# The weight sums of the first block of a retention and sliding-window kernel: made by GpSimd instead of VectorE

## The reference

```python
h = x @ ret_w_in                       # (2048, 6144): q, k, v, g
q, k = rope(q), rope(k) / 16           # 4 heads of 256
att = (q @ k.T) * dec                  # chunks of 64
r = att @ v + (q @ state) * xi         # v: 4 heads of 512
state = state * g_chunk + (k * zeta).T @ v
r = (r - mean(r)) * rsqrt(var(r) + GN_EPS)
x = post_norm(x, (silu(g) * r) @ ret_w_out)        # retention layer

kv = x @ swa_w_kv                      # one K/V, 4 heads of 64
q, gate = split(x @ swa_w_in)          # 16 heads of 64
p = softmax_with_sink(q @ k_band.T / 8 + bias)
x = post_norm(x, ((p @ v_band) * silu(gate)) @ swa_w_out)   # window layer
```

## Time and profile before

| | |
|---|---|
| median of 3 runs | 2483.75 us (2483.28 to 2490.3) |
| the profiled execution | 2483.47 us, its span 2481.5 us |
| PE, DVE, ACT, POOL busy | 2341.3, 1812.3, 1180.6, 345.5 us |
| share of the span | 94%, 73%, 48%, 14% |
| mean granted TensorE clock | 0.982 |

### The profile page before, as it was taken

How to read it: one execution, slowest core, us unless ns; L and a number is a source line. 1 busy time by engine, 2 the same in 40 slices (tenths; PEclk the granted TensorE clock), 3 DMA queues, 4 the chain that set the end, 5 groups by cost and what they waited for, 6 DMA issues and landing times.

```text
span 2481.5 us, 30993 instructions
## 1 busy us (share of the span) xinstructions
PE 2341.3 (94%) x11506; PEld 1900.2 (77%) x11506; DVE 1812.3 (73%) x2578; ACT 1180.6 (48%) x1754; POOL 345.5 (14%) x352
## 2 busy tenths in 40 slices
PE   7889989989999999999999999999999999999995
PEld 5677777867778887787778888778777888878774
DVE  6977888755886668874697767886478667787457
ACT  3433345346544445534744544443664445553473
POOL 4212201113001110001201001100110110010122
PEclk9999999999999999999999999999999999999998
DMA  9786677571764445744274544575146444464413
GB/s 331 280 294 246 226 240 254 170 280 52 241 199 148 135 129 173 263 148 136 91 268 134 170 158 131 168 256 185 62 153 237 131 141 154 128 203 134 131 60 110
DMA packets 215061, 443.38 MB, mean 179 GB/s; under 512 B 15040, under 2 KB 52432, under 8 KB 211328
## 3 DMA queue, kind: packets, MB, share of 16 engines
q1 hardware_dynamic: 200832, 375.58, 46.1%
q0 software_dynamic: 14080, 65.83, 7.2%
HBM read 379.75 MB, written 57.41 MB: 176 GB/s over the span
## 4 chain that ended last, share of the span: by engine, by line
PE 58%; DVE 15%; issue 12%; DMA 7%; ACT 4%; POOL 2%; SPq 1%; POOLq 0%; DVEq 0%; ACTq 0%
PE accs L644 16%; PE accs L645 15%; PE accs L646 15%; DVE w_lo L1250 5%; DMA stage<-t_prep 4%; PE bank L644 2%; PE bank L646 2%; PE bank L645 2%; ACT w_hi L948 2%; PE bank L866 1%; DMA x_sums<-part_lo 1%; PE bank L875 1%; PE bank L885 1%; PE bank L730 1%; POOL rstd L1830 1%
## 5 line engine op out<-in xcount | busy, mean ns | idle before, releaser
L1250 DVE TENSOR_TENSOR w_lo<-stage,w_hi 128x1024 fp32r<-128x1024 f32 x536 | 670.4, 1255 | 414.3 <-ACT w_hi L948 413.2
L948 ACT ACTIVATE w_hi<-stage 128x1024 fp32r<-128x1024 f32 x536 | 563.6, 1057 | 585.3 <-DMA stage<-t_prep 273.3
L644 PE MATMUL accs<-w_hi,xs 128*128 128x512 f32 x1120 | 450.5, 402 | 45.2 <-DVE krT L1328 12.0
L646 PE MATMUL accs<-w_hi,xs 128*128 128x512 f32 x1120 | 442.6, 395 | 0.0
L645 PE MATMUL accs<-w_lo,xs 128*128 128x512 f32 x1120 | 442.4, 395 | 0.0
L644 PEld LDWEIGHTS accs<-w_hi,xs 128*128 128x128 f32 x1120 | 214.1, 191 | 100.1 <-issue 51.5
L644 PE MATMUL accs<-x_hi,w_hi 128*128 128x512 f32 (+1 forms) x640 | 248.8, 389 | 17.4 <-DVE qT L1714 16.3
L1830 POOL TENSOR_TENSOR rstd<-ve,half 128x1 f32<-128x1 f32 x96 | 80.7, 841 | 1265.1 <-DVE ve L1306 1215.5
L646 PEld LDWEIGHTS accs<-w_hi,xs 128*128 128x128 f32 x1120 | 213.7, 191 | 46.3
L645 PEld LDWEIGHTS accs<-w_lo,xs 128*128 128x128 f32 x1120 | 214.1, 191 | 42.5
L645 PE MATMUL accs<-x_lo,w_hi 128*128 128x512 f32 (+1 forms) x640 | 239.9, 375 | 0.0
(11 more groups left out here) (184 smaller groups left out, 3863.9 us busy)
## 6 DMA issues: line engine op xcount, KB each, us to landing
stage<-t_prep SPq DMA_DIRECT2D x224, 512.0 KB, 4.4
stage<-ret_w_in SPq DMA_DIRECT2D x96, 512.0 KB, 3.9
stage<-ret_w_in SPq DMA_DIRECT2D x128, 256.0 KB, 2.9
stage<-swa_w_in SPq DMA_DIRECT2D x64, 512.0 KB, 3.8
t_prep<-t_buf POOLq DMA_DIRECT2D x28, 1024.0 KB, 6.3
stage<-ret_w_out SPq DMA_DIRECT2D x48, 512.0 KB, 3.7
cs<-rope_t SPq DMA_DIRECT2D x16, 1024.0 KB, 7.6
t_buf<-ret_w_in POOLq DMA_DIRECT2D x32, 512.0 KB, 9.6
```

The lines of the kernel that those rows point to most:

```text
L644: mm(dst, lhs[0], rhs[0], start=start, stop=False, skip_group_check=reopened)
L646: return mm(dst, lhs[1], rhs[0], start=False, stop=stop, skip_group_check=reopened)
L948: copy(w_hi[:, g % HS], stage[:, g % LS], ACT.Copy).then_inc(w_hi_made, 1)
L1250: nc.vector.tensor_tensor(w_lo[:, g % LS], stage[:, g % LS], w_hi[:, g % HS].bitcast(F32), sub).then_inc(w_split, 1)
```

## The change

The sums leave VectorE's program. GpSimd makes them with its own TENSOR_TENSOR, with the same operands, in the slot in which VectorE made them, and the store stands right behind each in the same slot instead of one slot later.

```diff
@@ block.vector
-            def make_t(n):
-                b = t_buf[T_BUF[n]]
-                dve.wait_ge(t_loaded[T_BUF[n]], 32 * T_NTH[n])
-                link(nc.vector.tensor_tensor(b[:, 1, 1, :], b[:, 1, 1, :], b[:, 0, 1, :], sub))
-                link(nc.vector.tensor_tensor(b[:, 0, 1, :], b[:, 0, 1, :], b[:, 0, 0, :], sub))
-                link(nc.vector.tensor_tensor(b[:, 0, 0, :], b[:, 1, 1, :], b[:, 0, 0, :], add))
-                nc.vector.tensor_tensor(b[:, 1, 0, :], b[:, 1, 0, :], b[:, 0, 0, :], sub).then_inc(t_made, 1)
...
-                    if s == 0:
-                        for n, _, _, at_slot in T_PLAN:
-                            if at_slot == p:
-                                make_t(n)
@@ block.gpsimd
+            def make_t(n):
+                b = t_buf[T_BUF[n]]
+                pool.wait_ge(t_loaded[T_BUF[n]], 32 * T_NTH[n])
+                link(tt(b[:, 1, 1, :], b[:, 1, 1, :], b[:, 0, 1, :], sub))
+                link(tt(b[:, 0, 1, :], b[:, 0, 1, :], b[:, 0, 0, :], sub))
+                link(tt(b[:, 0, 0, :], b[:, 1, 1, :], b[:, 0, 0, :], add))
+                tt(b[:, 1, 0, :], b[:, 1, 0, :], b[:, 0, 0, :], sub).then_inc(t_made, 1)
...
                         for n, _, at_slot, made in T_PLAN:
                             if at_slot == p:
                                 load_t(n)
-                            if made + 1 == p:
+                            if made == p:
+                                make_t(n)
                                 store_t(n)
```

## The result

The kernel after takes 2520.21 us (median of 4 runs, 2517.09 to 2526.72); the kernel before took 2483.52 beside it (4 runs, 2477.35 to 2490.3). The ratio is 1.0151, with a 95% interval of 1.0132 to 1.0171. The sign was right, the size almost three times too small, and 2520 lies above the range (2474 to 2512).

A forecast was written before the change was run, and what follows sets the result against it. TensorE bounds block 1; block 0 runs slower, with VectorE's sums and waits for DMA as suspects. The terms 16 + 5 + 0 + 4 + 2 - 8 - 6 = +13 on 2483.5 us gave 2497 us, range 2474 to 2512.

The forecast's parts named there:

- Start: Sets 0 to 3, made behind GpSimd's x sums, store set 3 late and delay TensorE's weights: +16 us.
- The blocking: GpSimd's SBUF reads and VectorE's two-input instructions run in turns; at the start it moves set 3's store from 56 to 62.5.
- the 10 named: Sign of being right: TensorE's wait before P6's second pair is over 10 us.
- Set 14: Made behind a GpSimd gate, its store lands later and ScalarE's copy_r waits 10 us or more: +5 us.
- Set 20: In the heads, its store now stands ahead of an inverse root and a gate, 0 to 2 us earlier: 0.
- Inverse roots: GpSimd's roots in block 0 come 0 to 3 us late in three or four places: +4 us.
- The third rival: GpSimd becomes the bound: late inverse roots in all heads, 3 to 5 us in ten places; 2520 us, chance 0.10.
- Transfers: Sets 9 to 11 and 14 to 16 are stored later, into the next head's loads: +2 us, bounds -3 and +6.
- VectorE in the heads: Twenty sets leave VectorE; of 3.0 us each, 1.5 to 2 return as blocking: -8 us, bounds 0 and -25.
- Last four: Sets 24 to 27 in the q slots are stored earlier and shorten TensorE's wait at the q copy: -6 us.
- DVE busy: Sign of being right: VectorE's busy time at about 1,750 to 1,780, not 1,728, because blocked time is counted.

The follow-up runs named there:

- h_after_store_later: The kernel after, with each set's store one slot later, as in the kernel before; 2518.3 us, ratio 1.0138.
- q_pool_nosums: s_heads_pool with the sums of sets 4 to 23 left out; GpSimd only waits for the loads and stores; 2487.44 us, ratio 0.9999.
- n_nosums: The kernel before, with VectorE's sums of sets 4 to 23 left out, loads and stores kept; 2474.31 us, ratio 0.9953.
- s_heads_pool: The kernel after, but only sets 4 to 23 made by GpSimd, the others by VectorE; 2500.16 us, ratio 1.0056.
- s_first4_dve: The kernel after, but sets 0 to 3 stay with VectorE, sets 4 to 27 on GpSimd; 2500.1 us, ratio 1.006.
- m_noread: s_heads_pool with four GpSimd memsets that read nothing in place of each set's sums, for sets 4 to 23; 2486.92 us, ratio 1.0018.

## Why the prediction was right in sign and wrong in size

**Start: right.** +16 forecast, +17.1 measured alone. The store of set 3 was forecast at 62.5 and came at 64.72; the wait behind it was 16.8 us, over the 10 named. The blocking, read from the earlier trace rows, was needed for that: without it the store comes at 58.

**Set 14: right that it costs, the size not settled.** +5 forecast; moving the set earlier wins 6.4 with real sums and 15.4 with memsets, and a part of either is the wait that the kernel before had too. From slot 38 to slot 48 the kernel after loses 7.1 us against the kernel before. The wait itself did not grow past 10 as written (7.97, from 6.75), since TensorE and ScalarE were late by then too; the cost showed in slots, not in the wait's row. Set 20, priced at 0, had a gain that was overlooked: ScalarE's wait of 7.26 us for its store is gone in the kernel after, which has this one wait left (waits view, 60 to 640 us):

```profile
ACT rT L1051 <- DMA t_prep<-t_buf: 8.0, 1, 8.0
```

**Inverse roots: wrong, small.** +4 forecast. Between 60 and 640 us VectorE does not wait for `rstd` at all, before or after. The third rival named 2520, the number that came, by late roots in all heads; that mechanism is refuted, and its number was luck.

**Transfers: not shown.** +2 forecast. No run takes them apart in the change: `h_after_store_later` moves all stores by a slot and differs by nothing that the intervals tell. `q_pool_nosums` loses 12 us against `n_nosums`, twice my upper bound, with the same bytes moved at other times; that the times of the transfers are the cause is argued there, not shown.

**VectorE in the heads: the step that failed.** I had each set give back 1.5 to 2 us of its 3.0 as blocked time. That was a little low: 2.0 go with the reads alone (39.7 us over 20 sets), and against 1812.3 less the sums it is 2.4 in `s_heads_pool` and 2.5 over all 28. But from it I concluded a net gain of 8 us, "at 40% of it". That treats 1 us of VectorE's freed time and 1 us of its blocked time as worth the same. They are not. The freed time was the sums at the end of the slot: 60 us of it are worth 11.7 (`n_nosums`), earlier stores included. The blocked time falls on `w_lo` and its like in the middle of the slot: 40 us of it, with GpSimd's own 17, cost 9.4 to 18.4. So the term is -1.5 (-10.9 + 9.4, with 15.4 for set 14 beside it) or +7.5 (-10.9 + 18.4, with 6.4 for set 14), in place of -8. Either way the sum is the 13.9 of `s_heads_pool`; the forecast's terms for the same sets, 5 + 4 + 2 - 8, gave 3.

**Last four: -6 forecast, -3.7 alone, nothing in the company of the rest** (`s_first4_dve`, which has them and the heads, costs 14.9 against the 13.9 of the heads alone). TensorE's wait at the q copy fell as forecast, under 6.

In all the missing 24 us are 11 in the heads, 7 at the last four, 1 at the start, and 5 by which the whole is more than its parts (within their intervals). The bounds of the heads' term were 0 and -25: it had no price above zero, and a net loss there, which `s_heads_pool` measures, had no place in the forecast's own range of 2487 to 2508. DVE busy came at 1797, above the forecast 1,750 to 1,780.

## What to carry to other kernels

Moving work off a busy engine is priced by what waits for the time freed, not by the busy time: here leaving 60 us of VectorE's work out wins 12, and moving it to GpSimd loses 14. Where two engines block one another, ask which instruction will be the one held up; here the sums at the end of VectorE's own slot came after the slot's `w_lo`, and the same sums on GpSimd held up the `w_lo` that TensorE needs. And look first at the fixed due times around the work: two slots for one set and one for another won 5.7 us without touching an engine.

## What the runs showed that I had not expected

An instruction of VectorE with one input was held up as well. VectorE's row of the cast `att_hi` in the kernel after, and GpSimd's around it (the first is the issue of two DMAs):

```profile
135.41 3.92 DVE L1392 CAST att_hi<-att 128x128 fp32r<-128x128 f32 x1
```
```profile
134.70 1.45 POOL L1775 DMA_DIRECT2D t_buf<-ret_w_in  x2
136.17 1.30 POOL L1831 TENSOR_TENSOR r_out<-r_out,sg 128x512 f32<-128x512 f32 x1
137.42 0.56 POOL L1826 TENSOR_TENSOR rstd<-ve,half 128x1 f32<-128x1 f32 x1
137.96 1.27 POOL L1831 TENSOR_TENSOR r_out<-r_out,sg 128x512 f32<-128x512 f32 x1
```

It takes 0.22 us at the median in the kernel before, and here it starts during the issue and ends 0.1 us behind the third GpSimd instruction after it. An issue alone seems to do it in the kernel before: the cast that starts at 173.59 takes 0.49 us and ends 0.05 us behind an issue of two loads (172.56 + 1.47). Memsets do it too: in `m_noread` a cast that starts in such an issue takes 1.93 us, to 175.11, where the first of three memsets ends by their mean at 175.04, and the mean of the 64 casts stays at 317 ns (321 after, 246 before), though `w_lo` is back at its old mean. So `m_noread` took most of the blocking away, not all. The Trainium skill, in the same section, counts the cast among the operations that can take the shared pair of ports; these rows agree, and I had weighed only the two-input half of that rule. In the row above TensorE did not wait for it.

Each store of GpSimd behind its own sum stands 0.30 us after the sum's end (`0.30 <-POOL t_buf L1784`, 28 times, 8.3 us in all). And GpSimd's busy time rose by 180.6 us (345.5 to 526.1) for 143 us of work, the other 38 being its own share of the blocking, about half of VectorE's 69.
